# Half a gate set ahead of the first hybrid scores, a fused final norm, zero products in three pauses, and an earlier gating at the FFN ends

## The chip, the cores and the metric

The kernel is one program on one core of one Trainium2 chip. The metric is the device time of one execution in microseconds (us), of which three were taken. Its engines work side by side and each takes its instructions in the order in which they are written: TensorE (PE: matrix products and transposes, called turns here), VectorE (DVE), ScalarE (ACT), GpSimd (POOL) and SyncE (SP, which issues most transfers from memory). They wait for one another by semaphores.

## The reference, cut to what matters

256 tokens of width 1024, in float32, go through two blocks, each of them a first FFN, a mixing of tokens by two attentions, and a second FFN; then a final norm, one hybrid layer, and a mixture of 32 experts.

```python
for l in range(2):
    x = x + 0.5 * g1 * swiglu(modulate(x, sh1, sc1), ...)     # FFN of width 2816
    x = x + g2 * token_mix(modulate(x, sh2, sc2), ...)
    x = x + 0.5 * g3 * swiglu(modulate(x, sh3, sc3), ...)
x = rms_norm(x) * final_norm

h = modulate_2(x, norm1_w, shift1, scale1)                    # the hybrid layer
x_in, conv_b, conv_c, q, k, v, f_logit, gate_conv_l, gate_attn_l = split(h @ w_in)
p_a = (conv_b * causal_depthwise_conv(conv_c * x_in, conv_w)) @ w_out_conv
p_b = forgetting_attention(rmsnorm(q), rmsnorm(k), v, log_sigmoid(f_logit + b)) @ w_out_attn
x = x + gate1 * ((sigmoid(gate_conv_l) * p_a + sigmoid(gate_attn_l) * p_b) @ w_o)

h2 = modulate_2(x, norm2_w, shift2, scale2)                   # the router and the experts
group = argmax(h2 @ w_rg); the two best experts of that group, weighted by softmax
x = x + gate2 * sum over experts of weight * ((silu(h2 @ w_gate) * (h2 @ w_up)) @ w_down)
```

## The kernel before

Every weight matrix is streamed from memory through `raw`, three blocks of 2048 columns for 128 partitions. Each block is split in halves of 1024 columns into a rounded part `w_hi` (ACT, L518) and the remainder `w_lo` (DVE, L986). The activations are split likewise (`uT_hi`, `uT_lo`), and `mm3` (L1849 to L1851) makes one float32 product out of three: w_hi by the high part, w_lo by the high part, w_hi by the low part. Nearly all of PE's work is such triples of 128 by 512. The order of everything is written by hand, engine by engine; semaphores with running counts link the engines (`x_ready` counts finished halves of `x`, `xn_done` scaled halves, `split_done` converted halves of weights).

**Norms.** ACT squares each of the four 128 by 512 parts of `x` (L535, two token tiles t by two halves h) and sums them; DVE adds two sums (`rms_sum`, L999), ACT takes the root (L539), DVE inverts it (`rms_inverse`, L1004) and scales the tile (`rms_scale`, L1010, two halves). PE turns the scaled tile into `bank` (L1892, 16 turns of 128 by 128), ACT and DVE apply scale and shift and split it (L568, L571, L1053, L1058), and the column products begin. While a norm runs, PE has nothing to do; `norm` on PE begins with `keep_warm(16, ...)`, 16 bfloat16 products of zeros by zeros, 128 by 512, into a bank that is not in use (L1839).

**FFN ends.** Four times a DVE function `x_update_ffn` multiplies four accumulated banks by the gate (L1103, L1121), adds them to `x` (L1104, L1124), and starts the next norm. Just ahead of it stands `h_tile(1)` (L1085), the low part of the last hidden tile.

**Final norm.** After the second block `x` is scaled by its own norm into `xn` (L1010) and multiplied by the rows of `final_norm` (L1532, 128 by 1024 for each tile); then the hybrid layer's own norm follows on the result.

**Hybrid layer.** After four column units of 768 and the forget gates come four gate sets of 512 columns (set 1: `hyb_gates(1)`, 8 values of k by 2 token tiles by 3 products, 48 products), and four attention jobs. `sc_job(j)` makes the scores of job j on PE (L2072, L2073), DVE adds a mask (L1269), ACT takes exponentials (L642), later PE turns and multiplies by the values. The order on PE ahead of the first job is: turns of q, k, the conv inputs (L2125), a wait for `kh_ready` (ACT's evicted k) and `uc_ready` (DVE's copy L1610 of the turned conv input), scores of job 0, the whole of set 1, scores of job 1, half of set 2. ACT takes the sigmoid of set 1 (L795) after the exponentials of job 0; set 2 writes to one of set 1's banks and waits for that.

**Router.** PE turns the logits (L2415), DVE picks the groups (L1687 to L1699), PE counts (L2419 to L2422), DVE builds 0/1 matrices `picks` (L1712), and PE gathers the chosen tokens by products with them (L2431, 32 products). The results go through DVE (L1664, L1673) to the first expert products; DVE also splits expert weights in between (L1723).

Of the kernel before, what the change touches and what calls it, by code (L numbers as in the profile page):

```python
# [33 lines left out]
T = S // P  # L34
D = 1024
KD = D // P
DEPTH = 2
# [59 lines left out]
def program(nc, stream, experts, ada, c_rows, consts, vecs, layer_vecs, cmp_w1, fnorm, x_in, out):  # L97
    ctx = ExitStack()
    with ctx:
# [290 lines left out]
        def gate_column(n, k):  # L390
            return modf[:, 16 + 8 * (n % 2) + k:17 + 8 * (n % 2) + k]

# [118 lines left out]
        def _(act):  # L511
# [355 lines left out]
            def token_hi(t):  # L867
                act.wait_ge(xn_done, 4 * (q6 + 2) + 2 * t + 2)
                act.activation(xn_hi[:, t], xn[:, t], ACT.Copy).then_inc(xn_hi_done, 1)
# [101 lines left out]
        def _(dve):  # L971
# [116 lines left out]
            def last_unit(u, f):  # L1088
                split(u, (2,), LAST_UNIT)
                hidden(f, (0,))  # L1090
                h_tile(0, (hL_hi_done, f // FFN_UNITS + 1), hL_ready)
                hidden(f, (1,))
                h_tile(1, (hT_hi_done, f + 1), hT_ready)

            def x_half(n, t, h, done):
                if (t, h) == (0, 0):
                    dve.wait_ge(gate_ready, n * 2 + 2)
                if (t, h) == (1, 1):
                    dve.wait_ge(*done)
                else:  # L1100
                    dve.wait_ge(first_tile, 3 * n + 2 * t + h + 1)
                c = slice(h * 512, (h + 1) * 512)
                link(V.tensor_tensor(upd[:, t, h], ACC[2 * t + h][:, :], gate_bc[:, c], ALU.mult))  # L1103
                V.tensor_tensor(x[:, t, c], x[:, t, c], upd[:, t, h], ALU.add).then_inc(x_ready, 1)  # L1104

# [8 lines left out]
            def x_update_ffn(n, done):  # L1114

                for t, h in ((0, 0), (0, 1), (1, 0)):
                    x_half(n, t, h, done)
                rms_sum(n + 1, 0)
                dve.wait_ge(*done)
                links[0] += 1  # L1120
                V.tensor_tensor(upd[:, 1, 1], ACC[3][:, :], gate_bc[:, 512:1024], ALU.mult).then_inc(chain, 1)  # L1121
                rms_inverse(n + 1, 0)
                dve.wait_ge(chain, links[1] + links[0])
                V.tensor_tensor(x[:, 1, 512:1024], x[:, 1, 512:1024], upd[:, 1, 1], ALU.add).then_inc(x_ready, 1)  # L1124
                rms_scale(n + 1, 0)

            def ffn1(l, u0, f0, n):
# [44 lines left out]
                x_update_ffn(stage, (used[2], u0 + n + 1))  # L1172

            def ffn2(l, u0, f0, n):
# [46 lines left out]
                x_update_ffn(stage, (used[2], u0 + n + 1))  # L1221
# [304 lines left out]
            q6, n6 = 3 * DEPTH, 3 * DEPTH  # L1526
            dve.wait_ge(c_landed, DEPTH * 32 + 32)
            for t in range(T):
                if t > 0:
                    norm_tile(q6, t)  # L1530
                dve.wait_ge(xn_done, 4 * q6 + 2 * t + 2)
                V.tensor_tensor(x[:, t], xn[:, t], fn_bc, ALU.mult).then_inc(x_ready, 2)  # L1532
# [294 lines left out]
        def _(pe):  # L1827
# [55 lines left out]
            def norm(n, q):  # L1883
                keep_warm(16, GU[0][:, :])
                pe.wait_ge(x_ready, 4 * q + 4)
                for t in range(T):
                    for b in range(4):
                        if b % 2 == 0:
                            pe.wait_ge(xn_done, 4 * q + 2 * t + b // 2 + 1)
# [416 lines left out]
            norm(n6, n6 + 1)  # L2306
            for m in range(4):
# [65 lines left out]
            m.then_inc(b_psum, 1)  # L2373
            pe.wait_ge(kh_ready, 2)
            pe.wait_ge(uc_ready, 1)

            def first():
                pe.wait_ge(fcum_ready, 1)
                hyb_gates(1)
# [37 lines left out]

            pe.wait_ge(sel_ready, 1)
# [3 lines left out]
            pe.matmul(ACC[1][:, 0:4], ones, g_sel[:, 1], start=False, stop=True, skip_group_check=True).then_inc(count_psum, 1)  # L2422
            pe.wait_ge(gate_ready, 2 * n6 + 4)
# [271 lines left out]
```

## Time and profile before

| | |
|---|---|
| device time, median of 3 | 1802.78 us (1800.56 to 1805.46) |
| the profiled execution: its time | 1803.52 us |
| its span in the trace | 1801.7 us |
| mean granted TensorE clock over the span | 0.987 of full |
| PE busy | 1727.0 us, 96% |
| DVE, ACT busy | 1368.1 us (76%), 967.6 us (54%) |
| chain of work that ended last | PE 83%, DVE 9%, ACT 5% |

An engine is busy while an instruction of its own runs. A share near 100% on PE means that other engines' work hides behind it nearly everywhere; the chain's 9% of DVE and 5% of ACT are the places where it does not. The granted clock is the share of full speed at which TensorE was let run in a stretch; 0.50 and 1.00 are its two levels, 1.2 and 2.4 GHz.

### The profile page before, as it was taken

What the parts mean: (1) busy time and instruction counts of PE and PEld (TensorE: products, weight loads), DVE (VectorE), ACT (ScalarE), POOL (GpSimd) and SP (SyncE); (2) the same over time, 40 slices, a digit from 0 to 9 for tenths busy, and PEclk for the clock granted to TensorE, in tenths of its full rate; (3) what the DMA queues carried; (4) which work ended last, traced back from release to release, by engine and by line L of the source; (5) the groups of instructions that cost most, each with busy time, mean ns of one, the idle gap of its engine ahead of it and who ended that gap; (6) DMA issues with size and microseconds to landing.
All of it is one profiled execution on the core that took longest, in us unless ns stands there. A gap on an engine that the chain in (4) does not pass through costs nothing.

```text
span 1801.7 us, 24959 instructions
## 1 busy us (share of the span) xinstructions
PE 1727.0 (96%) x8653; PEld 1406.2 (78%) x8653; DVE 1368.1 (76%) x2069; ACT 967.6 (54%) x1471; POOL 47.0 (3%) x92
## 2 busy tenths in 40 slices
PE   5999999999999999999989999999899998999998
PEld 3788878787788878887878878888687876888886
DVE  6887777766876678777687578876767578999997
ACT  3444464664644454445546655444535547777775
POOL 0000000000000000000000000000000000000000
PEclk8999999999999999999999999999898999999999
DMA  8988754225577759886622348887373444999994
GB/s 362 355 329 307 297 198 147 71 95 209 208 282 249 266 193 340 301 310 231 234 82 106 112 169 306 343 306 276 143 296 114 187 164 147 382 353 354 369 353 164
DMA packets 61802, 437.43 MB, mean 243 GB/s; under 512 B 6816, under 2 KB 7328, under 8 KB 9504
## 3 DMA queue, kind: packets, MB, share of 16 engines
q1 hardware_dynamic: 47504, 339.27, 50.0%
q0 software_dynamic: 12672, 92.28, 13.7%
q10 hardware_dynamic: 1552, 4.89, 0.8%
q8 instruction: 47, 0.77, 0.2%
q14 instruction: 27, 0.22, 0.0%
HBM read 435.36 MB, written 1.05 MB: 242 GB/s over the span
## 4 chain that ended last, share of the span: by engine, by line
PE 83%; DVE 9%; ACT 5%; issue 1%; DMA 1%; ACTq 0%; SPq 0%; DVEq 0%
PE bank L1849 25%; PE bank L1850 24%; PE bank L1851 24%; DVE w_lo L986 2%; PE bank L2095 2%; ACT w_hi L518 1%; PE bank L2113 1%; DVE ada_w L1018 1%; PE bank L1939 1%; PE bank L2075 1%; DVE arena L1325 1%; PE bank L2073 1%; PE bank L2431 1%; ACT arena L535 1%; PE bank L2069 1%
## 5 line engine op out<-in xcount | busy, mean ns | idle before, releaser
L986 DVE TENSOR_TENSOR w_lo<-raw,w_hi 128x1024 fp32r<-128x1024 f32 x426 | 501.8, 1221 | 201.3 <-ACT w_hi L518 200.2
L518 ACT ACTIVATE w_hi<-raw 128x1024 fp32r<-128x1024 f32 x426 | 426.6, 1052 | 333.8 <-PE bank L1851 330.5
L1849 PE MATMUL bank<-w_hi,uT_hi 128*128 128x512 f32 (+2 forms) x1408 | 551.4, 392 | 22.4 <-DVE uT_lo L1342 13.4
L1850 PE MATMUL bank<-w_lo,uT_hi 128*128 128x512 f32 (+2 forms) x1408 | 539.2, 383 | 0.0
L1851 PE MATMUL bank<-w_hi,uT_lo 128*128 128x512 f32 (+2 forms) x1408 | 538.2, 382 | 0.0
L1849 PEld LDWEIGHTS bank<-w_hi,uT_hi 128*128 128x128 f32 x1408 | 266.9, 190 | 81.3 <-DVE uT_lo L1342 15.4
L1851 PEld LDWEIGHTS bank<-w_hi,uT_lo 128*128 128x128 f32 x1408 | 266.7, 189 | 52.1
L1850 PEld LDWEIGHTS bank<-w_lo,uT_hi 128*128 128x128 f32 x1408 | 267.3, 190 | 47.2
L1849 PE MATMUL bank<-w_hi,r_arena 128*128 128x512 f32 (+1 forms) x744 | 294.7, 396 | 5.0 <-DVE r_arena L1747 2.5
L1850 PE MATMUL bank<-w_lo,r_arena 128*128 128x512 f32 (+1 forms) x744 | 290.9, 391 | 0.0
L1851 PE MATMUL bank<-w_hi,r_arena 128*128 128x512 f32 (+1 forms) x744 | 289.8, 390 | 0.0
L1018 DVE CUSTOM_DVE_ANT_0 ada_w<-ada_w,cmpw 128x1024 f32<-128x1024 f32 x176 | 207.1, 1220 | 8.1 <-DMA ada_w<-ada_pairs 7.8
L1849 PEld LDWEIGHTS bank<-w_hi,r_arena 128*128 128x128 f32 x744 | 139.8, 188 | 37.4 <-DVE r_arena L1747 3.2
L1851 PEld LDWEIGHTS bank<-w_hi,r_arena 128*128 128x128 f32 x744 | 139.7, 188 | 29.6
L1850 PEld LDWEIGHTS bank<-w_lo,r_arena 128*128 128x128 f32 x744 | 140.0, 188 | 26.7
L993 DVE TENSOR_TENSOR w_lo<-raw,w_hi 128x1024 fp32r<-128x1024 f32 x94 | 110.9, 1222 | 9.0 <-ACT w_hi L526 7.1
L526 ACT ACTIVATE w_hi<-raw 128x1024 fp32r<-128x1024 f32 x94 | 94.1, 1052 | 14.3 <-PE bank L1851 14.3
L584 ACT ACTIVATE arena<-bank 128x256 f32<-128x256 f32 x88 | 33.8, 386 | 120.6 <-PE bank L1851 120.6
L488 POOL DMA_DIRECT2D ada_w<-ada_pairs x88 | 46.8, 532 | 1290.0 <-DVE mods_gate L1018 555.2
L993 DVE TENSOR_TENSOR w_lo<-ada_w,w_hi 128x1024 fp32r<-128x1024 f32 x60 | 70.6, 1222 | 4.8 <-ACT w_hi L526 3.9
L526 ACT ACTIVATE w_hi<-ada_w 128x1024 fp32r<-128x1024 f32 x64 | 64.1, 1053 | 7.6 <-PE bank L1851 7.6
L642 ACT ACTIVATE arena<-arena,stat 128x256 f32<-128x256 f32 (+1 forms) x112 | 49.4, 444 | 19.0 <-DVE stat L1274 18.9
(339 smaller groups left out, 1461.5 us busy)
## 6 DMA issues: line engine op xcount, KB each, us to landing
raw<-weight_stream SPq DMA_DIRECT2D x216, 1024.0 KB, 4.9
ada_w<-ada_pairs POOLq DMA_DIRECT2D x88, 1024.0 KB, 5.2
raw<-expert_blocks SPq DMA_DIRECT2D x48, 1024.0 KB, 4.8
ada_w<-expert_blocks SPq DMA_DIRECT2D x32, 1024.0 KB, 4.9
cmpw<-expert_blocks SPq DMA_DIRECT2D x16, 1024.0 KB, 5.0
arena<-ada_pairs SPq DMA_DIRECT2D x5, 1024.0 KB, 13.1
ada_w<-ada_pairs SPq DMA_DIRECT2D x3, 1024.0 KB, 13.4
cmpw<-compress_w ACTq DMA_DIRECT2D x2, 1024.0 KB, 7.9
```

The costliest lines, as they stand in the source:

```text
L488: pool.dma_start(ada_w[:, slot], ada[g]).then_inc(ada_landed[slot], 16)
L518: act.activation(w_hi[:, b], v, ACT.Copy).then_inc(hi_done, 1)
L526: act.activation(w_hi[:, b], v, ACT.Copy).then_inc(hi_done, 1)
L584: act.activation(act_g[:, t], GU[t][:, 0:F_UNIT], ACT.Silu).then_inc(silu_done, 1)
L642: e = act.activation(v, v, ACT.Exp, bias=nmax[j % 2][:, h:h + 1], accum_out=psum_row[j % 4][:, h:h + 1])
L986: V.tensor_tensor(w_lo[:, b], v, f32(w_hi[:, b]), ALU.subtract).then_inc(split_done, 1)
L993: V.tensor_tensor(w_lo[:, b], v, f32(w_hi[:, b]), ALU.subtract).then_inc(split_done, 1)
L1018: e = V.tensor_tensor_reduce(w[:, i], w[:, i], c, 1.0, 0.0, ALU.mult, ALU.add, dst[:, i:i + 1])
L1849: pe.matmul(dst, xh, w_hi[:, off:off + n], start=first, stop=False, skip_group_check=True)
L1850: pe.matmul(dst, xh, w_lo[:, off:off + n], start=False, stop=False, skip_group_check=True)
L1851: return pe.matmul(dst, xl, w_hi[:, off:off + n], start=False, stop=last, skip_group_check=True)
L2095: m = pe.matmul(HT[:, a * DH:(a + 1) * DH], pT[j % 2][:, kt, a], v, start=kt == 0, stop=kt == qt, skip_group_check=True)
```

## The change

It has five parts.

- Hybrid attention, PE: the first half of gate set 1 (k 0 to 3, 24 products) goes ahead of the waits for `kh_ready` and `uc_ready` and of job 0's scores; the second half stays behind those scores.
- Final norm, DVE: one instruction for each half, x times the inverse root times the row (`final_half`), takes the place of the scaling into `xn` and of the multiplication. The second tile's sum and inversion stand between these halves. The counts of `xn_done` drop by four from there on.
- The pause of that norm, PE: after the 16 zero products three times seven more, each seven released by `x_ready` (after the first, second and fourth half), and five more behind the turns.
- Router, PE: nine zero products ahead of the wait for the groups, eight ahead of the wait for the picks.
- FFN ends, DVE: the multiplication by the gate for the part (0, 0) goes ahead of `h_tile(1)`.

```diff
+        def scaled(q):
+            return 4 * (q - (q > 3 * DEPTH))
...
             def token_hi(t):
-                act.wait_ge(xn_done, 4 * (q6 + 2) + 2 * t + 2)
+                act.wait_ge(xn_done, scaled(q6 + 2) + 2 * t + 2)
...
-                h_tile(1, (hT_hi_done, f + 1), hT_ready)
-
-            def x_half(n, t, h, done):
+
+            def gated(n, t, h, done):
                 if (t, h) == (0, 0):
                     dve.wait_ge(gate_ready, n * 2 + 2)
                 if (t, h) == (1, 1):
                     dve.wait_ge(*done)
                 else:
                     dve.wait_ge(first_tile, 3 * n + 2 * t + h + 1)
+                links[0] += 1
+                V.tensor_tensor(upd[:, t, h], ACC[2 * t + h][:, :], gate_bc[:, h * 512:(h + 1) * 512], ALU.mult).then_inc(chain, 1)
+
+            def added(t, h):
+                dve.wait_ge(chain, links[1] + links[0])
                 c = slice(h * 512, (h + 1) * 512)
-                link(V.tensor_tensor(upd[:, t, h], ACC[2 * t + h][:, :], gate_bc[:, c], ALU.mult))
                 V.tensor_tensor(x[:, t, c], x[:, t, c], upd[:, t, h], ALU.add).then_inc(x_ready, 1)
+
+            def x_half(n, t, h, done):
+                gated(n, t, h, done)
+                added(t, h)
...
-            def x_update_ffn(n, done):
-
-                for t, h in ((0, 0), (0, 1), (1, 0)):
+            def x_update_ffn(n, f, done, last=False):
+
+                gated(n, 0, 0, done)
+                h_tile(1, (hT_hi_done, f + 1), hT_ready)
+                added(0, 0)
+                for t, h in ((0, 1), (1, 0)):
                     x_half(n, t, h, done)
                 rms_sum(n + 1, 0)
-                dve.wait_ge(*done)
-                links[0] += 1
-                V.tensor_tensor(upd[:, 1, 1], ACC[3][:, :], gate_bc[:, 512:1024], ALU.mult).then_inc(chain, 1)
+                gated(n, 1, 1, done)
                 rms_inverse(n + 1, 0)
-                dve.wait_ge(chain, links[1] + links[0])
-                V.tensor_tensor(x[:, 1, 512:1024], x[:, 1, 512:1024], upd[:, 1, 1], ALU.add).then_inc(x_ready, 1)
-                rms_scale(n + 1, 0)
+                added(1, 1)
+                if not last:
+                    rms_scale(n + 1, 0)
...
-                x_update_ffn(stage, (used[2], u0 + n + 1))
+                x_update_ffn(stage, f0 + n - 1, (used[2], u0 + n + 1), last=l == DEPTH - 1)
...
             q6, n6 = 3 * DEPTH, 3 * DEPTH
+            def final_half(t, h):
+                c = slice(h * 512, (h + 1) * 512)
+                V.scalar_tensor_tensor(x[:, t, c], x[:, t, c], rstd[:, t:t + 1], fn_bc[:, c], ALU.mult, ALU.mult).then_inc(x_ready, 1)
+
             dve.wait_ge(c_landed, DEPTH * 32 + 32)
-            for t in range(T):
-                if t > 0:
-                    norm_tile(q6, t)
-                dve.wait_ge(xn_done, 4 * q6 + 2 * t + 2)
-                V.tensor_tensor(x[:, t], xn[:, t], fn_bc, ALU.mult).then_inc(x_ready, 2)
+            dve.wait_ge(rstd_done, 2 * q6 + 1)
+            dve.wait_ge(x_ready, 4 * q6 + 2 + 2)
+            final_half(0, 0)
+            rms_sum(q6, 1)
+            final_half(0, 1)
+            rms_inverse(q6, 1)
+            dve.wait_ge(rstd_done, 2 * q6 + 2)
+            final_half(1, 0)
+            final_half(1, 1)
             dve.wait_ge(x_ready, 4 * (q6 + 2))
             norm(q6 + 1, n6, late=HYB_U0)
...
             def norm(n, q):
                 keep_warm(16, GU[0][:, :])
+                if q == 3 * DEPTH + 1:
+                    for h in (1, 2, 4):
+                        pe.wait_ge(x_ready, 4 * q + h)
+                        keep_warm(7, GU[0][:, :])
                 pe.wait_ge(x_ready, 4 * q + 4)
                 for t in range(T):
                     for b in range(4):
                         if b % 2 == 0:
-                            pe.wait_ge(xn_done, 4 * q + 2 * t + b // 2 + 1)
+                            pe.wait_ge(xn_done, scaled(q) + 2 * t + b // 2 + 1)
...
             norm(n6, n6 + 1)
+            keep_warm(5, GU[0][:, :])
...
             m.then_inc(b_psum, 1)
+            pe.wait_ge(fcum_ready, 1)
+            hyb_gates(1, range(4))
             pe.wait_ge(kh_ready, 2)
             pe.wait_ge(uc_ready, 1)
 
             def first():
-                pe.wait_ge(fcum_ready, 1)
-                hyb_gates(1)
+                hyb_gates(1, range(4, KD))
...
+            keep_warm(9, GU[0][:, :])
             pe.wait_ge(sel_ready, 1)
...
+            keep_warm(8, GU[0][:, :])
             pe.wait_ge(gate_ready, 2 * n6 + 4)
```

Line numbers differ between the two programs: L1849 to L1851 (`mm3`) are L1868 to L1870 after it, L2125 (a turn) is L2148, L2072 and L2073 (scores) are L2095 and L2096, L1839 (zeros) is L1858.

On PE, at the hybrid's first scores, the rows before were these: the last turns of the conv inputs, job 0's scores, and the first product of set 1.

```order
L2125 MATMUL bank<-cst,arena 128x128 x8
L2072 MATMUL bank<-r_arena 128x256
L2073 MATMUL bank<-cmpw 128x256
...
L1849 MATMUL bank<-w_hi,uT_hi 128x512
L1850 MATMUL bank<-w_lo,uT_hi 128x512
```

On PE, in the same place, they are now these; the three rows of a triple stand eight times ahead of the first scores.

```order
L2148 MATMUL bank<-cst,arena 128x128 x8
L1868 MATMUL bank<-w_hi,uT_hi 128x512
L1869 MATMUL bank<-w_lo,uT_hi 128x512
L1870 MATMUL bank<-w_hi,uT_lo 128x512
...
L2095 MATMUL bank<-r_arena 128x256
L2096 MATMUL bank<-cmpw 128x256
```

What moved is the eight rows of scores: behind 24 products.

On DVE, at the final norm, before: the last halves of `x`, the scaling into `arena` (which holds `xn`), the product with the row, and the second tile.

```order
L1124 TENSOR_TENSOR x<-x,arena 128x512
L1010 TENSOR_SCALAR arena<-x,stat 128x512 x2
L1522 MEMSET stat 128x1
L1532 TENSOR_TENSOR x<-arena 128x1024
L999 TENSOR_TENSOR stat<-stat 128x1
L1004 RECIPROCAL stat<-stat 128x1
L1010 TENSOR_SCALAR arena<-x,stat 128x512 x2
L1532 TENSOR_TENSOR x<-arena 128x1024
L999 TENSOR_TENSOR stat<-stat 128x1
```

On DVE, there now (L1110 adds, L1540 is `final_half`, L1002 and L1007 are the sum and the inversion):

```order
L1110 TENSOR_TENSOR x<-x,arena 128x512
L1533 MEMSET stat 128x1
L1540 SCALAR_TENSOR_TENSOR x<-x,stat,arena 128x512
L1002 TENSOR_TENSOR stat<-stat 128x1
L1540 SCALAR_TENSOR_TENSOR x<-x,stat,arena 128x512
L1007 RECIPROCAL stat<-stat 128x1
L1540 SCALAR_TENSOR_TENSOR x<-x,stat,arena 128x512 x2
L1002 TENSOR_TENSOR stat<-stat 128x1
```

Four products of 512 columns stand where four scalings and two products of 1024 columns stood.

## Rows read from the trace of the kernel before

**Rows 1.** The page: busy time per engine, and TensorE's granted clock in 40 slices.
```profile
PE 1727.0 (96%) x8653; PEld 1406.2 (78%) x8653; DVE 1368.1 (76%) x2069; ACT 967.6 (54%) x1471; POOL 47.0 (3%) x92
...
PEclk8999999999999999999999999999898999999999
```

**Rows 2.** Timeline of PE at the hybrid's start: start, duration, [idle before <-releaser].
```profile
1266.05 3.63 PE L1839 MATMUL bank<-zeros 128*128 128x512 bf16 x16
...
1275.32 3.65 PE L1892 MATMUL bank<-cst,arena 128*128 128x128 f32 x16 [5.65 <-DVE arena L1010]
...
1286.01 0.40 PE L1849 MATMUL bank<-w_hi,uT_hi 128*128 128x512 f32 x1
```

**Rows 3.** Windows: PE busy (count) first, granted clock third from last; hybrid's start, first FFN end.
```profile
1266.00:1269.70 3.70, 3.67 (x17) 1.47 (x16) 3.17 (x9) 2.86 (x9) 0.00 (x0) 1.00 0.40 142
...
1275.30:1279.00 3.70, 3.65 (x16) 3.15 (x16) 2.48 (x7) 1.37 (x5) 0.00 (x0) 0.50 0.00 0
...
235.60:238.60 3.00, 2.79 (x24) 2.35 (x22) 2.04 (x5) 1.37 (x3) 0.00 (x0) 1.00 0.00 0
```

**Rows 4.** Timeline of DVE at the final norm and the hybrid's first norm.
```profile
1268.27 0.67 DVE L1124 TENSOR_TENSOR x<-x,arena 128x512 f32<-128x512 f32 x1
...
1273.97 0.16 DVE L999 TENSOR_TENSOR stat<-stat 128x1 f32<-128x1 f32 x1
...
1276.44 0.88 DVE L1010 TENSOR_SCALAR arena<-x,stat 128x512 f32<-128x512 f32 x2
```

**Rows 5.** Groups by form: busy and mean ns of one multiply-and-multiply on 256 columns.
```profile
L1619 DVE SCALAR_TENSOR_TENSOR arena<-arena,vec 128x256 f32<-128x256 f32 x8 | 3.3, 480 | 0.1
```

**Rows 6.** Timeline of DVE, ACT and PE at the first FFN's end.
```profile
229.50 0.69 DVE L1104 TENSOR_TENSOR x<-x,arena 128x512 f32<-128x512 f32 x1
...
231.73 0.61 ACT L535 ACTIVATE arena<-x 128x512 f32<-128x512 f32 x1
...
236.14 0.88 DVE L1010 TENSOR_SCALAR arena<-x,stat 128x512 f32<-128x512 f32 x2
...
244.17 0.50 PE L1849 MATMUL bank<-w_hi,uT_hi 128*128 128x512 f32 x1
```

**Rows 7.** Timeline of PE around the first hybrid scores and gate set 1.
```profile
1371.85 0.35 PE L2072 MATMUL bank<-r_arena 128*128 128x256 f32 x1 [1.65 <-DVE arena L1610]
...
1378.26 0.79 PE L1849 MATMUL bank<-w_hi,uT_hi 128*128 128x512 f32 x1
...
1391.21 0.28 PE L2072 MATMUL bank<-r_arena 128*128 128x256 f32 x1
...
1394.86 0.50 PE L1849 MATMUL bank<-w_hi,uT_hi 128*128 128x512 f32 x1
```

**Rows 8.** Windows inside gate set 1, columns as in rows 3.
```profile
1378.20:1382.20 4.00, 4.00 (x10) 3.14 (x10) 4.00 (x7) 1.36 (x2) 0.00 (x0) 0.50 0.00 0
...
1382.20:1391.20 9.00, 9.00 (x40) 7.37 (x39) 6.45 (x11) 3.37 (x9) 0.00 (x0) 0.99 0.35 117
```

**Rows 9.** Timeline of DVE and ACT in the same stretch.
```profile
1381.20 1.65 DVE L1269 SCALAR_TENSOR_TENSOR arena<-bank,arena,cst 128x256 f32<-128x256 f32 x4
...
1386.24 1.28 ACT L795 ACT_TABLE_LOAD   x1
...
1391.41 1.09 ACT L795 ACTIVATE arena<-bank 128x512 f32<-128x512 f32 x2 [3.88 <-PE bank L1851]
```

**Rows 10.** Timeline of PE at the router and the gather.
```profile
1493.42 0.39 PE L2419 MATMUL bank<-arena,cst 128*128 128x8 f32 x2 [1.96 <-DVE arena L1697]
...
1496.41 0.76 PE L2431 MATMUL bank<-picks,xn_hi 128*128 128x512 f32 x1 [1.94 <-issue]
...
1508.13 0.47 PE L1849 MATMUL bank<-w_hi,r_arena 128*128 128x512 f32 x1 [1.60 <-DVE r_arena L1673]
```

**Rows 11.** Waits of DVE during the gather: us in total, times, longest.
```profile
DVE arena L1664 <- PE bank L2431: 2.2, 3, 1.0
```

**Rows 12.** Window of the gather's first products, columns as in rows 3.
```profile
1496.40:1501.60 5.20, 5.19 (x12) 4.11 (x13) 4.54 (x14) 1.72 (x4) 0.00 (x0) 0.50 0.01 3
```

More of the change, by code:

```diff
@@ L1171, in ffn1 @@
                 last_unit(u0 + n - 1, f0 + n - 1)
-                x_update_ffn(stage, (used[2], u0 + n + 1))
+                x_update_ffn(stage, f0 + n - 1, (used[2], u0 + n + 1))
             def ffn2(l, u0, f0, n):
@@ L1220, in ffn2 @@
                 last_unit(u0 + n - 1, f0 + n - 1)
-                x_update_ffn(stage, (used[2], u0 + n + 1))
+                x_update_ffn(stage, f0 + n - 1, (used[2], u0 + n + 1), last=l == DEPTH - 1)
             def merge(u0, m, stage, gates, following, between, more=True):
```

## The prediction

> **What bounds the kernel now.** I read the page first: PE is busy for 1727.0 of 1801.7 us and its granted clock is at its upper level in nearly all of the 40 slices; the reader is to see the three slices that stand at 8 [rows 1]. Outside them there is little to win that is not fewer products. Two of them, 1261 to 1306 and 1351 to 1396 us, lie past the second block; the first is the kernel's start, which the change leaves alone. So I read the timelines of PE and DVE there and at the router, where the change also works, for pauses of PE and the clock behind each.
>
> Three places answer. At the hybrid's start PE runs out of zero products at 1266.05 + 3.63 = 1269.68 and waits till 1275.32 for a scaled tile, 5.65 us [rows 2]; the turns behind the pause run at the lower level (0.50), while zero products just ahead of it ran at 1.00, and turns at the first FFN's end, without such a pause, ran at 1.00 too [rows 3]. In the attention PE waits 1.65 us, then runs job 0's scores and the first part of set 1 at the lower level. At the router two pauses of about 2 us stand ahead of a gather that begins at the lower level. In all three PE is what ends last afterwards.
>
> **The change part by part.** The sum is made against the profiled execution, 1803.52 us, with 1.8 us around its span; it is 0.74 above the median of 1802.78.
>
> *Final norm.* DVE adds the last part of x till 1268.27 + 0.67 = 1268.94, and reaches the first sum of the next norm at 1273.97, 5.03 us later [rows 4]. In between now stand four products by a scalar and a row, a sum, an inversion. The trace has no such product of 512 columns. One of 256 columns takes 0.48 us [rows 5], so twice that, 0.96, bounds it above; a plain 512-column addition takes 0.67 [rows 4], which bounds it below. I take 0.75, nearer to the addition, since a fixed part is counted twice in 0.96. Four of them are 3.0, and the sum between them about 0.16 as in [rows 4]: the next sum then starts at about 1272.1, 1.9 earlier (2.2 with 0.67, 1.0 with 0.96). The inversion waits for ACT's root, but behind the second product, by which time it is done. **−1.9.**
>
> *Zero products there.* Twenty-one more, at 3.63/16 = 0.227 us each [rows 2], are 4.8 us. The first seven start when the first product is out, near 1269.7, as the sixteen end; the next follow without a gap, and the last seven start behind the fourth half, at some 1272.7, and end near 1274.3. The first scaled half would be there near 1273.4, so its turns start late by up to 0.9; but the second tile comes at 1276.44 − 1.9 + 0.5 = 1275.0 at the earliest, and eight turns of the first fit ahead of it at full clock. I charge **+0.1**. What is bought is the clock: from the scaling of the second tile to the first product of k = 2 it was 1286.01 − 1276.44 = 9.57 us [rows 2, 4]; the same path, with the same shapes, at the first FFN's end was 244.17 − 236.14 = 8.03 [rows 6], at full clock. **−1.5.** The product of k = 2 waits for converted weights at either place, so no more than this is to be had. The five products behind the turns lie in the pause for ACT and DVE, at nothing; without that cover they would be 1.1.
>
> *Half a set ahead of the scores.* Before: scores of job 0 from 1371.85 to 1378.26, 6.41 us; set 1 till 1391.21; scores of job 1 till 1394.86, 3.65 us at full clock [rows 7]. Inside set 1 the first 4 us ran at 0.50, and then 40 products took 9.00, 0.225 each [rows 8]. Now the products can start where PE stopped, 1371.85 − 1.65 = 1370.2; their weights are converted, since no wait stood ahead of them at 1378.26. 24 products make 5.5 us (till 1375.7), the scores 3.65 (till 1379.4), the rest of the set 5.5 (till 1384.9), job 1's scores 3.65 (till 1388.6). The pause is filled, and nothing behind it is slow: PE reaches set 2 about 6.2 earlier. Who else must keep up: DVE's mask of job 0 starts at 1381.20 behind its own work, whether the scores are there at 1378.3 or 1379.4, and so ACT's exponentials and table load stay: the load ends at 1386.24 + 1.28 = 1387.5, and the sigmoids, which waited 3.88 us for PE, take 1.09, till 1388.6 [rows 9]. Set 2 needs their bank. Both chains meet at about 1388.75. **−6.1**; DVE and ACT have no slack left there, so what is lost in either counts from now on. Queued behind the moved products are the scores alone, and DVE would wait for those only if they came after 1381.2.
>
> *Router.* Nine zero products, 2.0 us, stand in a pause of 1.96, eight, 1.8, in one of 1.94 [rows 10]: up to 0.1 late in the first, nothing in the second. The gather's first 12 products then take 12 × 0.225 = 2.7 in place of 5.2 us [rows 8, 12], 2.5 earlier. DVE, which takes in the gather, waited for it 2.2 us in three pieces [rows 11]; when these are gone DVE is the chain, so 2.2 is the limit. First expert product at 1505.9 instead of 1508.13 [rows 10]. **−2.2.**
>
> *FFN ends.* The multiplication starts up to 0.7 earlier on DVE (the length of such an instruction, [rows 6]), but the next norm goes by ACT: at the first end the first half of x was ready at 229.50 + 0.69 = 230.19, and ACT, busy with a conversion and a table load, squared it from 231.73 [rows 6]. DVE would wait for it. **0**; if it paid in full, four times that, 2.8.
>
> *Sum.* −1.9 + 0.1 − 1.5 − 6.1 − 2.2 = −11.6, so 1803.52 − 11.6 = **1791.9 us**. The stages behind each place run on PE with hardly a pause, so the gains should carry to the end.
>
> A rule of the Trainium skill speaks against the second and third term. "TensorE: Matmul & The Clock Gate", Part 4, says that the full clock does not engage for transpose-mode work, which does not count as busy the same way. The trace agrees in one place, where 16 turns in 3.65 us did not lift the clock from 0.50, and not in the other, where 24 turns and products at 235.6 kept it at 1.00 [rows 3]. By that rule the turns ahead of set 1 would drop the clock, and the time would be that of the first rival.
>
> **The rivals.**
> 1. *The clock falls during the turns ahead of set 1 all the same.* The products moved up would then run at 0.50. If it recovers after 4 us, as inside set 1 [rows 8], 2 us of the 6.1 are lost: 1793.9. If it takes all of the 10.4 us from 1371.85 to 1382.2 that it took before [rows 7, 8], 5.2 are lost: 1797.1. For it: turns did not lift the clock [rows 3]. Against it: they kept it at 235.6, and now no pause follows them. 15%, near 1795.
> 2. *The zero products do not hold the clock.* They then take twice as long, 0.45 each, and PE is late itself: at the norm 21 of them are 9.5 us from 1269.7, so turns start at 1279.2 instead of 1275.32, though then without the saving of 1.9; at the router the 17 are 7.7 in 3.9 of pause. That is +3.9 + 3.8 − 6.1 = +1.6: 1805. Against it: at 1266 to 1269.7 they ran at 1.00 [rows 3]. 5%.
> 3. *The attention gives part back.* DVE or ACT, without slack at 1388.6, or weights not converted in time for set 2, keep 3 to 4 of the 6.1: about 1795. For it: both chains already end where PE's does; against it: ACT's sigmoids waited 3.88 us for PE alone [rows 9]. 12%.
> 4. *The other side: the clock stays down through all of set 1 and both jobs' scores.* At the lower level a product takes about 0.42 [rows 8] and a job's scores 6.41: 48 × 0.42 + 12.8 = 33.0 from 1370.2, so 1403.2 instead of 1394.86, +8.3; with −5.5 from the rest 1806.3, slower than before. It decides if the clock is low at 1370 and not lifted within about 28 us of such work; before, it was lifted after 10.4. 4%.
> 5. *The FFN ends pay in full:* 1789.1. 4%.
>
> **How the numbers follow.** My forecast has 60%, its own range 1789.5 to 1794 (the product's two bounds, 0.3 less or 0.9 more, a spread of the runs of about 2). A measurement of this kernel can tell about 0.3%, 5.4 us, from no change; faster thus means below 1797.4. The forecast, rivals 1, 3 and 5 lie there, 91%, less some 7% for their upper tails and a run that falls high: 0.84. Rivals 2 and 4 lie within 0.3% above, with those tails: 0.13; 0.03 for slower. The range 1788.5 to 1798 leaves out rivals 2 and 4 and small tails.
>
> **What would show it.** Right: granted clock 1.00 in the turns of the hybrid's start and in the first 12 gather products; the next norm's first sum 3.2 us behind the last addition; a first product of set 1 0.1 us behind the turns, at 0.225 a product, scores of job 0 in 3.65; set 2 some 18.5 us behind those turns; first expert product 9.5 us behind the start of the gather; FFN ends as long as before. Wrong: a pause of PE ahead of set 2 for ACT's sigmoid, products at 0.42 behind the turns, zero products that end after what they wait for, or a new wait for weights in set 2 or in the merge, which would give the 6.1 back.

## The result, and the profile after

The changed kernel takes 1794.44 us (median of 6, 1787.76 to 1798.63) against 1802.79 us (6, 1800.56 to 1805.46): ratio 0.9946, 95% interval 0.9933 to 0.9960, 0.54% faster. The forecast was 1791.9 us, range 1788.5 to 1798.0. The profiled execution took 1796.7 us, its span is 1795.0 us at a mean granted clock of 0.991.

The page of the changed kernel, busy time of the engines and the clock in 40 slices: the two later slices that stood at 8 [rows 1] stand at 9.

```profile
PE 1733.0 (97%) x8696; PEld 1407.6 (78%) x8696; DVE 1365.8 (76%) x2067; ACT 967.5 (54%) x1471; POOL 46.9 (3%) x92
...
PEclk8999999999999999999999999999999999999999
```

**Hybrid's start.** The timeline of PE:

```profile
1266.78 8.32 PE L1858 MATMUL bank<-zeros 128*128 128x512 bf16 x37
1274.93 1.91 PE L1915 MATMUL bank<-cst,arena 128*128 128x128 f32 x16
1276.68 1.24 PE L1858 MATMUL bank<-zeros 128*128 128x512 bf16 x5
1278.66 0.47 PE L1868 MATMUL bank<-w_hi,uT_hi 128*128 128x512 f32 x1 [0.74 <-DVE uT_lo L1061]
...
1283.24 0.50 PE L1868 MATMUL bank<-w_hi,uT_hi 128*128 128x512 f32 x1
```

and that of DVE (the last addition, the first fused half, the next norm's first sum, its second scaling):

```profile
1268.77 0.67 DVE L1110 TENSOR_TENSOR x<-x,arena 128x512 f32<-128x512 f32 x1
...
1269.58 0.75 DVE L1540 SCALAR_TENSOR_TENSOR x<-x,stat,arena 128x512 f32<-128x512 f32 x1
...
1272.62 0.16 DVE L1002 TENSOR_TENSOR stat<-stat 128x1 f32<-128x1 f32 x1
...
1275.09 0.88 DVE L1013 TENSOR_SCALAR arena<-x,stat 128x512 f32<-128x512 f32 x2
```

The pause of 5.65 us and the slow turns [rows 2] are gone: 37 zero products lead into 16 turns that take 1.91 us together. From the first zero product to the first product of k = 2 it is 16.46 us against 19.96 before [rows 2], 3.5 less.

**Attention.** The timeline of PE and ACT from the last turns of the conv inputs to the first product of set 2, which answers to [rows 7, 9]:

```profile
1366.41 1.10 PE L2148 MATMUL bank<-cst,arena 128*128 128x128 f32 x8 [0.34 <-ACT cmpw L837]
...
1367.26 0.48 PE L1868 MATMUL bank<-w_hi,uT_hi 128*128 128x512 f32 x1
...
1372.82 0.28 PE L2095 MATMUL bank<-r_arena 128*128 128x256 f32 x1
...
1382.09 0.28 PE L2095 MATMUL bank<-r_arena 128*128 128x256 f32 x1
...
1384.83 1.08 ACT L798 ACTIVATE arena<-bank 128x512 f32<-128x512 f32 x2
...
1386.02 0.57 PE L1868 MATMUL bank<-w_hi,uT_hi 128*128 128x512 f32 x1 [0.20 <-issue]
...
1426.62 0.48 PE L1868 MATMUL bank<-w_hi,r_arena 128*128 128x512 f32 x1
```

The last row is the first product of the merge, the stage behind the attention. In the trace of before, the start of the same turns and the merge's first product were these:

```profile
1369.10 1.10 PE L2125 MATMUL bank<-cst,arena 128*128 128x128 f32 x8 [0.34 <-ACT cmpw L834]
...
1430.88 0.48 PE L1849 MATMUL bank<-w_hi,r_arena 128*128 128x512 f32 x1
```

Set 2 starts 19.61 us behind the start of those turns; before it was 1394.86 − 1369.10 = 25.76 (the product is in [rows 7]). That is 6.15 less. ACT's sigmoid now ends at 1385.91, just ahead of set 2, and PE is idle for 0.20 there.

Then comes what the forecast did not have. Windows of the changed kernel; the columns are busy time and count of PE, PEld, DVE, ACT, POOL, then the granted clock, and DMA:

```profile
1274.90:1276.70 1.80, 1.80 (x18) 1.75 (x17) 1.43 (x4) 0.20 (x1) 0.00 (x0) 1.00 0.00 0
1367.30:1385.80 18.50, 18.50 (x74) 12.63 (x72) 17.87 (x33) 8.95 (x17) 0.00 (x0) 1.00 0.31 118
1386.00:1389.40 3.40, 3.38 (x9) 2.62 (x10) 3.37 (x6) 1.81 (x2) 0.00 (x0) 0.54 0.00 0
1393.20:1406.70 13.50, 13.50 (x78) 11.22 (x76) 6.22 (x12) 11.39 (x24) 0.00 (x0) 1.00 0.39 144
1406.80:1413.50 6.70, 6.70 (x17) 5.20 (x17) 5.43 (x9) 3.94 (x6) 0.00 (x0) 0.50 0.04 5
1492.10:1496.00 3.90, 3.87 (x17) 3.18 (x18) 3.69 (x13) 2.53 (x5) 0.00 (x0) 1.00 0.00 0
```

The clock is at its upper level in the turns, in half a set, the scores and the other half, and in the gather. But behind the scores of job 1 and the idle 0.20 us it falls for 3.4 us, and during the scores of job 3 for 6.7 us, there with PE busy without a break ahead of it (13.50 of 13.50 us). Such a stretch at the lower level is called a drop from here on. By the lengths and levels of these rows the two cost about 1.6 and 3.3 us (an estimate). From the turns' start to the merge's first product it is 60.21 us instead of 61.78: of 6.15 us gained at set 2, 1.57 are left.

**Router.** The timeline of PE, which answers to [rows 10], from the logits' turns on:

```profile
1486.87 0.31 PE L2440 MATMUL bank<-cst,arena 36*128 36x36 f32 x2
1487.11 2.12 PE L1858 MATMUL bank<-zeros 128*128 128x512 bf16 x9
...
1490.06 1.89 PE L1858 MATMUL bank<-zeros 128*128 128x512 bf16 x8
1492.13 0.47 PE L2458 MATMUL bank<-picks,xn_hi 128*128 128x512 f32 x1 [0.19 <-issue]
...
1501.41 0.47 PE L1868 MATMUL bank<-w_hi,r_arena 128*128 128x512 f32 x1 [1.59 <-DVE r_arena L1692]
```

From the gather's start to the first expert product it is 9.28 us instead of 11.72. From the logits' turns it is 14.54 instead of 16.98 (they start at 1491.15 in the trace of before), 2.4 less. DVE no longer waits for the gather.

**The books.** In the profiled pair the three places give 3.5 + 6.15 + 2.4 = 12.1 us. 4.6 go back behind set 2, and 0.7 before the hybrid layer, where this execution had clock drops near 383 and 937 us and that of before one near 72: 6.8, against a difference of the spans of 6.7. Span times (1 − clock) is 1801.7 × 0.013 = 23.4 us before and 1795.0 × 0.009 = 16.2 after, which comes near the difference of the spans. It does not show that the clock is all of it: the shorter final norm and the pause ahead of the scores (1.9 and 1.65 us) were idle time of PE, and kernel e1 below has a span 3.9 us shorter than before at the same clock, 0.987. Among executions of one kernel the two do go together: those of the changed kernel had spans from 1786.1 us at 0.996 to 1797.0 at 0.990.

### The profile page after: what moved, and what is told of

Read it like the earlier page. It is cut to its first block, busy times and chain, and to the rows that moved or that the text cites. A ratio compares the mean times of both kernels' runs of the same rounds, so it can differ in the third digit from the quotient of the medians.

```text
span 1795.0 us, 25042 instructions
## 1 busy us (share of the span) xinstructions
PE 1733.0 (97%) x8696; PEld 1407.6 (78%) x8696; DVE 1365.8 (76%) x2067; ACT 967.5 (54%) x1471; POOL 46.9 (3%) x92
## 4 chain that ended last, share of the span: by engine, by line
PE 84%; DVE 9%; ACT 5%; issue 1%; DMA 1%; ACTq 0%; SPq 0%; DVEq 0%
PE bank L1868 25%; PE bank L1869 24%; PE bank L1870 24%; DVE w_lo L989 2%; PE bank L2118 2%; ACT w_hi L521 1%; PE bank L2136 1%; PE bank L1858 1%; DVE ada_w L1021 1%; PE bank L1962 1%; PE bank L2098 1%; DVE arena L1336 1%; PE bank L2092 1%; PE bank L2096 0%; ACT arena L538 0%
## 5 line engine op out<-in xcount | busy, mean ns | idle before, releaser
L1868 PE MATMUL bank<-w_hi,uT_hi 128*128 128x512 f32 (+2 forms) x1408 | 552.4, 392 | 21.5 <-DVE uT_lo L1353 12.9
L1870 PE MATMUL bank<-w_hi,uT_lo 128*128 128x512 f32 (+2 forms) x1408 | 539.0, 383 | 0.0
L1868 PEld LDWEIGHTS bank<-w_hi,uT_hi 128*128 128x128 f32 x1408 | 267.5, 190 | 81.2 <-DVE uT_lo L1353 14.9
L1870 PEld LDWEIGHTS bank<-w_hi,uT_lo 128*128 128x128 f32 x1408 | 266.9, 190 | 52.3
L1868 PE MATMUL bank<-w_hi,r_arena 128*128 128x512 f32 (+1 forms) x744 | 294.6, 396 | 5.0 <-DVE r_arena L1766 2.5
L1870 PE MATMUL bank<-w_hi,r_arena 128*128 128x512 f32 (+1 forms) x744 | 289.9, 390 | 0.0
L1868 PEld LDWEIGHTS bank<-w_hi,r_arena 128*128 128x128 f32 x744 | 139.7, 188 | 37.4 <-DVE r_arena L1766 3.2
L1870 PEld LDWEIGHTS bank<-w_hi,r_arena 128*128 128x128 f32 x744 | 139.7, 188 | 29.5
L1858 PE MATMUL bank<-zeros 128*128 128x512 bf16 x239 | 56.7, 389 | 5.9 <-DMA cst<-shape_constants 5.9
## 6 DMA issues: line engine op xcount, KB each, us to landing
ada_w<-ada_pairs SPq DMA_DIRECT2D x3, 1024.0 KB, 13.5
```

The costliest lines, as they stand in the source:

```text
L1858: pe.matmul(dst, zeros[:, 0:P], zeros[:, 0:dst.shape[1]], start=True, stop=True, skip_group_check=True)
L1868: pe.matmul(dst, xh, w_hi[:, off:off + n], start=first, stop=False, skip_group_check=True)
L1870: return pe.matmul(dst, xl, w_hi[:, off:off + n], start=False, stop=last, skip_group_check=True)
```

## The experiments

Two theories stood after the result. **Theory 1:** the terms are right, and the drops behind set 2 are chance, as others are in other stages. **Theory 2:** the new order brings them, because PE now reaches stretches of scores, turns and value products at another moment. "Old order" is job 0's scores ahead of all of set 1, as before; "new order" is half of set 1 first. In the old order the clock is low from the pause ahead of the scores into set 1 [rows 8]; its return there is called the recovery. Each kernel below was run against before on its own chip; "turns to merge" is the time from the start of the last turns of the conv inputs to the merge's first product, in the trace of each.

**One part at a time.** Each has only its piece of the diff above; e12 is the change without the first of its five parts.

> Only the half gate set ahead of the first hybrid scores is made, all else as before. Theory 1 (the terms add up, and the 4.6 us given back later in the attention are chance drops of the clock): from the last turns of the conv inputs to the first product of set 2 the time falls from 25.8 to about 19.6 us, median 5 to 6 us below before, and drops of the clock behind set 2 are seen in some kernels and not in others. Theory 2 (the moved products themselves bring the drops at the scores of jobs 1 and 3): the same 6 us at set 2, but the granted clock falls to 0.50 behind the scores again, and the median is only 1 to 2 us below before.

> Only the fused final norm and its zero products are made. Theory 1: the last FFN product to the first product of k = 2 goes from 20.2 to about 16.7 us, granted clock 1.00 in the turns, median 3 to 4 us below before; the attention's pause and its slow scores stay as before. Theory 2 (drops come from the moved attention products): the same, and no drop in the later attention.

> Only the zero products in the router's two pauses are made. Both theories: the gather's first 12 products at full clock, logits' turns to first expert product 17.0 to 14.5 us, median about 2.4 us below before. A rival, that zero products do not hold the clock there, gives 17.0 to some 18.5 and a slower kernel.

> Only the earlier gating at the four FFN ends is made. Theory 1: ACT sets the next norm, so DVE waits longer for its squares (0.9 instead of 0.4 us) and the median stays within 1 us of before. Rival: it pays in full, 2 to 2.8 us below before.

> The whole change but the half gate set ahead of the first scores, which stays in the old order. Theory 2 (in the new order the later scores let the clock fall, in the old order they do not): no drop after the recovery inside set 1, as in the four traces of the old order so far; from the last turns of the conv inputs to the merge's first product 60 to 62 us; and the median only 1.5 to 4.6 us above the changed kernel's 1794.4 to 1794.9, so 1796 to 1799.5. Theory 1 (the drops are chance in either order): drops after set 1 in this trace too, or a median 6 us above, 1800 to 1801.

| kernel | median, us (n) | before there, us (n) | ratio, interval |
|---|---|---|---|
| e1, attention alone | 1799.68 (11) | 1803.75 (35) | 0.9980 (0.9967 to 0.9993) |
| e2, final norm and its zeros alone | 1801.75 (12) | 1803.75 (35) | 0.9990 (0.9975 to 1.0005) |
| e3, router alone | 1799.93 (12) | 1803.75 (35) | 0.9982 (0.9970 to 0.9995) |
| e4, FFN ends alone | 1805.92 (11) | 1803.75 (35) | 1.0009 (0.9994 to 1.0023) |
| e12, all but the attention | 1800.08 (12) | 1802.18 (17) | 0.9983 (0.9971 to 0.9995) |

The places do in each what they did together. e2: first zero product to k = 2, 16.69 us. e3: logits' turns to first expert product, 14.55. e1: set 2 after 21.02 us and not 19.6, as both theories had it, because of a drop already inside the second half of set 1 (from 1378.3 us); a second one follows from 1388.6 us, and turns to merge are 58.46 us, 3.3 less than before. The medians of e1 and e2 fell by 4.1 and 2.0 us, less than the changed kernel's gains in these places (6.15 up to set 2, 3.3 for the norm); for e2 the interval still holds the 3.3, for e1 it ends at 6.0 (1803.75 × 0.0033). e3's median fell by 3.8, more than the 2.4 of its place, which its interval holds.

e4's timeline of DVE, last FFN end:

```profile
1265.94 0.16 DVE L999 TENSOR_TENSOR stat<-stat 128x1 f32<-128x1 f32 x1 [0.87 <-ACT arena L535]
```

DVE waits 0.87 us for ACT's squares, as foreseen. From the first zero product to the first column product it is 7.63 us at the first end and 8.14 at the second, as before; at the last 14.09 against 14.32. The median's rise of 2.2 us is not told from none by its interval, and nothing in the trace speaks for it.

e12 tells on the order. Its window behind the recovery, columns as above:

```profile
1386.00:1430.00 44.00, 43.52 (x221) 34.99 (x220) 23.94 (x42) 25.67 (x48) 0.00 (x0) 1.00 0.36 139
```

No drop, as in the four other traces of the old order. Its median, though, is 5.2 to 5.6 above the changed kernel's two medians (1794.44, and 1794.87 in e6): above theory 2's 1796 to 1799.5, and at the lower end of theory 1's 1800 to 1801. The trace speaks for theory 2, the median for theory 1. So the size of what is given back is left open by the medians; the ratios put the worth of the moved half set in the full change at 5 to 7 us, in e1 at 4, with intervals of 2 to 3 us on each.

**Without the zero products** (the lines `keep_warm(7/5/9/8, ...)` taken out of the changed kernel):

```diff
-                if q == 3 * DEPTH + 1:
-                    for h in (1, 2, 4):
-                        pe.wait_ge(x_ready, 4 * q + h)
-                        keep_warm(7, GU[0][:, :])
...
-            keep_warm(5, GU[0][:, :])
...
-            keep_warm(9, GU[0][:, :])
...
-            keep_warm(8, GU[0][:, :])
```

> The whole change without its zero products (those of the final norm's pause, the five behind the turns, the seventeen of the router). Theory 1 (the zero products are what holds the clock): turns and first column products at the hybrid's start and the first 12 gather products at 0.50 again, 1.5 and 2.2 us lost, so a median 3 to 4 us above that of the changed kernel. Rival (the shorter norm and the moved products alone would have held it): clock 1.00 in both places, median within 1 us of the changed kernel.

1797.05 us (5), ratio 0.9964 (0.9951 to 0.9977). The timeline of PE at the hybrid's turns and the gather:

```profile
1270.67 3.65 PE L1911 MATMUL bank<-cst,arena 128*128 128x128 f32 x16 [3.57 <-DVE arena L1013]
...
1488.80 0.77 PE L2451 MATMUL bank<-picks,xn_hi 128*128 128x512 f32 x1 [1.94 <-issue]
```

and the windows of the two:

```profile
1270.70:1274.30 3.60, 3.60 (x16) 3.10 (x16) 2.43 (x7) 1.27 (x5) 0.00 (x0) 0.50 0.00 0
1488.80:1493.60 4.80, 4.80 (x11) 3.79 (x12) 4.13 (x14) 1.71 (x4) 0.00 (x0) 0.50 0.01 3
```

The fused norm cuts the pause to 3.57 us, and the clock falls all the same; the turns take 3.65 us again and the gather starts slow. So the zero products hold the clock, and all traces agree: at the hybrid's start the clock is low in all five without them (before, e1, e3, e4, e5) and in none of the nine with them, and at the gather in all five without them (before, e1, e2, e4, e5) and in none of the nine with them. Without them the median is 2.2 to 2.6 us higher, less than the 3 to 4 expected, with intervals that overlap. Why it is less is not shown; e5's trace has no drops in the mixing stages, where the changed kernel's first trace has three, but its second (e6, below) has none either.

**The changed kernel once more.**

> The changed kernel once more, unaltered, for a second trace. Theory 1 (chance drops): other places than 380, 935, 1386 and 1407 us show drops in part, the span less the clock's deficit is again near 1778 us, and single executions lie between 1787 and 1799. Theory 2 (the moved products bring the drops): a drop behind the scores of job 1 or job 3 again.

1794.87 us (6), ratio 0.9956 (0.9942 to 0.9970). Near 383, 937 and 1003 us there is no drop this time, and one near 72; behind set 2 there is one again, at 1404 us, in the scores of job 3, and none behind those of job 1. The first part is theory 1's, the second theory 2's: that a drop comes in the new order repeats, and behind which scores does not.

**Scores among gate products.** In the hybrid layer, the scores of a job and the gate products beside them are interleaved:

```diff
+                        if amid:
+                            amid[2 * p + i]()
...
-                        sc_job(j0, jobs, j + 1)
-                        beside(j)
+                        sc_job(j0, jobs, j + 1, amid(j) if amid else ())
+                        if not (amid and j):
+                            beside(j)
...
-                hyb_gates(1, range(4, KD))
+                hyb_gates(1, (4, 5))
...
+                if j == 0:
+                    return [lambda: hyb_gates(1, (6,)), lambda: None, lambda: hyb_gates(1, (7,)), lambda: None]
...
+                return [lambda i=i: chunk(i) for i in range(4)]
```

`amid` is called behind each fourth of a job's scores; `chunk(i)` makes the products of one k of set 2 or 3.

> The changed kernel with the scores of hybrid jobs 1, 2 and 3 spread among the gate products beside them (a fourth of a job's scores, then one k, and so on), the same instructions in number. Theory 2 (runs of scores without dense products between them let the clock fall now that PE reaches them at another moment): no drops between 1376 and 1425 us, deficit 2 to 4 us smaller, median 2 to 4 us below the changed kernel. Theory 1: drops as often as before, there or elsewhere, median within 1 us.

1795.26 us (6), ratio 0.9961 (0.9948 to 0.9974): no gain, where theory 2 expected 2 to 4 us, and turns to merge 61.09 us. There is no drop from 1376 to 1414 us, as theory 2 had it, but the waits of PE from 1350 to 1440 us show why it does not pay (us in total, times, longest):

```profile
PE bank L2121 <- DVE arena L1302: 2.3, 1, 2.3
PE bank L2095 <- DVE arena L1280: 0.7, 1, 0.7
```

Job 3's scores end so late that the last value products wait 2.3 us for DVE, and right behind that wait the clock falls once. The next kernel spreads less: job 1 half its scores, k 7, the other half; job 2 as here; job 3 half, one k, half, three k.

> The changed kernel with scores spread among gate products so that no value product waits: job 1's first half, one k, second half; job 2's fourths with a k behind each; job 3's first half, one k, second half, three k. The 3 us of new waits seen where all three jobs were spread should be gone (PE's wait of 2.3 us for DVE ahead of the last value products, 0.7 ahead of job 1's scores). Theory 2 (scores without dense products between them let the clock fall): from the last turns of the conv inputs to the merge's first product 55 to 57 us against 57.1 to 60.2, median 2 to 3 us below the changed kernel. Theory 1 (chance): 57 to 60 as before, median within 1 us.

1792.28 us (6), ratio 0.9941 (0.9926 to 0.9956). The windows of this kernel that answer to the second to fifth of the changed kernel's:

```profile
1367.30:1385.80 18.50, 18.50 (x75) 12.63 (x73) 17.80 (x33) 8.94 (x17) 0.00 (x0) 1.00 0.31 118
1386.00:1422.00 36.00, 35.41 (x191) 29.35 (x192) 21.11 (x38) 23.74 (x47) 0.00 (x0) 1.00 0.42 160
```

The clock stays up through all of it, and turns to merge take 55.63 us: with the same products, 6.15 less than before, so that here the whole gain at set 2 reaches the merge. The median is 2.2 to 2.6 below the changed kernel's, at the foot of theory 2's 2 to 3; the intervals overlap, the traces do not. The table goes up to the merge; drops are counted behind the recovery in the old order, behind the start of set 1 in the new.

| order in the attention | kernels | drops | turns to merge, us |
|---|---|---|---|
| old | before, e2, e3, e4, e12 | none in 5 | 60.27 to 61.81 |
| new | changed, e1, e5, e6, e8, e10 | in all 6 | 56.92 to 60.21 |
| new, scores of jobs 1 to 3 spread evenly | e7 | one, behind the wait of 2.3 us | 61.09 |
| new, scores spread as in e9 | e9, e11 | none in 2 | 55.63, 55.68 |

The idle 0.20 us ahead of set 2 is a rival for the changed kernel's first drop: there PE waits for ACT's sigmoid. e10, described below, speaks against it. Its windows from behind the start of the turns up to a drop in job 1's scores, and behind it:

```profile
1363.50:1381.70 18.20, 18.20 (x75) 12.67 (x72) 17.54 (x33) 8.63 (x17) 0.00 (x0) 1.00 0.32 121
1381.80:1385.10 3.30, 3.27 (x9) 2.32 (x8) 3.22 (x8) 2.24 (x3) 0.00 (x0) 0.50 0.00 0
```

The clock fell while the scores ran, with PE busy in all of the 18.20 us ahead; and e9 has an idle 0.18 us ahead of set 2 and no drop.

**The mixing stages' pauses.** The same two means, products moved into a pause and zero products, where drops were seen in some traces, near 318, 385, 937 and 1003 us:

```diff
+                        if j == 9:
+                            keep_warm(6, SPARE[:, :])
                         pe.wait_ge(w_evac_a, l * 9 + 5 + j // 3)
-                    for i, k in GATE_CHUNKS[j]:
+                    for i, k in GATE_CHUNKS[j][(1 if j == 0 else 0):]:
...
+                def ahead():
+                    pe.wait_ge(km_ready, l * 4 + 4)
+                    gate_chunk(*GATE_CHUNKS[0][0])
+
-                jobs_run(l * NJ, l * 6, JOBS, beside, ending=lambda: turn_o((0, 1)))
+                jobs_run(l * NJ, l * 6, JOBS, beside, first=ahead, ending=lambda: turn_o((0, 1)))
```

> The changed kernel with the two mixing stages treated alike: the first gate chunk of six products goes ahead of the scores of job 1 (a pause of 1.7 us there), six zero products ahead of the wait for ACT's sigmoid at job 9 (a pause of 1.6 us). If the drops near 318, 385, 935 and 1000 us come from these pauses: none there any more, and with 1.3 us of pause filled by real work in each of two layers a median 4 to 6 us below the changed kernel. If they do not come from the pauses: 2 to 3 us below at most.

1788.66 us (5), ratio 0.9918 (0.9906 to 0.9931), 6.2 below the changed kernel on the same chip, and the intervals do not meet; expected were 4 to 6 if the pauses bring the drops. The timeline of PE in the first layer, scores of job 0, the moved chunk, scores of job 1:

```profile
317.99 1.14 PE L2098 MATMUL bank<-arena 64*128 64x256 f32 x8
319.49 0.50 PE L1868 MATMUL bank<-w_hi,uT_hi 128*128 128x512 f32 x1 [0.36 <-DVE cmpw L1498]
...
321.10 1.14 PE L2098 MATMUL bank<-arena 64*128 64x256 f32 x8
```

Of the pause of 1.7 us 0.36 is left, and no drop is in either mixing stage of this trace, nor of those of e10 and e11, which have the same edit. Of the eleven traces without it seven have one to three there and four (e1, e5, e6, e7) none, so the median says more here than one trace.

**And the first FFN's pause**, eleven zero products ahead of the loop of the first FFN:

```diff
                 down(u0, f0)
+                if nn == 0:
+                    keep_warm(11, SPARE[:, :])
```

> The kernel of the mixing pauses with eleven zero products more, ahead of the loop of the very first FFN, where PE waits 2.6 to 3.2 us for DVE and the clock then fell near 72 us in seven of nine traces. If that pause is the cause: no drop there, 1 to 1.7 us below the kernel of the mixing pauses. If the zeros end late or the drop comes from the stretch before: the same or 0.5 us slower.

1789.65 us (5), ratio 0.9925 (0.9911 to 0.9939). The window just behind that pause, first in e8, then here:

```profile
70.00:75.00 5.00, 4.72 (x16) 4.01 (x17) 5.00 (x8) 0.60 (x1) 0.53 (x1) 0.66 0.81 269
```

```profile
70.00:75.00 5.00, 4.65 (x23) 3.92 (x24) 5.00 (x8) 0.60 (x1) 0.53 (x1) 1.00 0.81 288
```

The drop is gone in the trace, as in that of e11; of the twelve traces without this edit nine have it. The median does not show a gain (0.99 above e8, intervals overlapping).

**All of it.**

> All of it: the changed kernel, the mixing pauses, the first FFN's pause and the spread scores. By theory 2 the gains add: 4 to 5 us (mixing) + 1 to 1.7 + 2 to 3 below the changed kernel, near 1785 to 1787. By theory 1 the spread scores add nothing: 1787 to 1789.

1786.02 us (5, 1785.34 to 1788.53), ratio 0.9909 (0.9895 to 0.9922): faster than before and than the changed kernel (0.9946, 0.9933 to 0.9960). From e10 it differs by the spread scores alone: on the same chip the median is 3.63 us lower, and four of its five executions lie below all five of e10's, though the intervals of the ratios still overlap. By its expectation this is theory 2's time (1785 to 1787) and not theory 1's (1787 to 1789). The window over all but the start and the end:

```profile
45.00:1780.00 1735.00, 1703.37 (x8604) 1388.19 (x8622) 1336.76 (x2009) 950.57 (x1442) 45.58 (x87) 1.00 0.65 242
```

The clock is at 1.00 throughout, and the five executions lie within 3.2 us, where those of the changed kernel lie within 10.9.

## Why the prediction was right, and where it was not

Time, sign and range held; the likeliest value was 2.5 us too low. The median also lies 0.4 us above the range that the forecast gave to its own case (1789.5 to 1794), next to the "about 1795" of rival 3. The range was wide enough for a loss that the prediction did not name, but single executions, from 1787.76 to 1798.63, reach beyond both of its ends, so that chance had a part in it. Step by step:

- *Final norm, −1.9.* The new instruction takes 0.75 us, the value chosen between 0.67 and 0.96. Last addition's end to the next sum: 3.18 us instead of 5.03. Right.
- *Zero products there, +0.1 and −1.5.* From the second scaling to k = 2 it is 8.15 us, against 8.03 expected and 9.57 before: −1.42 together. e5 shows that they, and not the shorter pause, hold the clock. Right.
- *Attention, −6.1.* At set 2: −6.15, with ACT's sigmoid just ahead of it, as worked out. The step that failed is the sentence that "the gains should carry to the end": between the first scores and the merge the new order has clock drops in six of six traces, and the old one none in five. Of the 6.1 there were left 1.6 (changed kernel) to 4.9 us (e10) at the merge, and all of it in e9, without drops. "Nothing behind it is slow" held for the changed kernel up to set 2; in e1 and e5 a drop came right behind job 0's scores, and the gain at set 2 was 4.7 to 4.9. Rival 3 had the outcome (part given back) and the wrong cause: it named DVE, ACT and weights. That runs of scores without dense products between them have a part in the drops is shown by e9 and e11, where spreading them took the drops away with no product less. They are not enough by themselves: the old order has the same run of job 1's scores, 3.65 us, and no drop behind it in five traces. Why is not settled, and the medians leave open how much the drops cost in the mean.
- *Router, −2.2.* −2.44, 0.2 more than DVE's waits, which the prediction took as the limit; these waits are gone, as was said. Right.
- *FFN ends, 0.* At the first three nothing; at the last 0.23. Right.
- *Rival 1* did not happen: the turns ahead of set 1 kept 1.00 in every trace of the new order, so the rule of the Trainium skill weighed there ("TensorE: Matmul & The Clock Gate", Part 4), by which they would have cost 2 to 5 us, is not borne out in this place. *Rival 2:* the zeros held the clock everywhere. *Rival 4:* no. *Rival 5:* no, by e4.

The prediction also read from the page that there was little to win outside the slices that stand at 8. e8 won 6.2 us in slices that stand at 9: a drop of 3.4 us inside a slice of 45 us leaves it at 9. And the forecast took the profiled execution as typical for what it does not touch. Executions differ by whole drops, each some 1.7 us (an estimate: 3.4 us at half the clock), near 72, 318, 385, 937 and 1003 us; that made the medians of single parts (e1, e2, e4) poor measures, where the traces' distances were good ones.

## What to carry to other kernels

Where PE is the bound, a change's gain is held only as long as the clock is: look with windows at every stretch behind the edit in which PE is busy with small products, scores or transposes, and not at its pauses alone. Real work moved into a pause fills it and took the drops away here, zero products only hold the clock, and both pay if they fit; spreading small products among dense ones costs nothing as long as the small ones' consumers still get them in time (e7 against e9). Compare such kernels by distances within traces and by the granted clock, since single executions differ by more than a part is worth.

## What the runs showed of the hardware

The granted clock fell to 0.50 with PE busy without a break ahead: in e10 from 1381.7 us, behind 18.2 us of unbroken work, the last 3.4 of it scores, and in the changed kernel from 1406.7 us, behind 13.5 us of turns, value products, scores and gate products. "Busy" in the profile is therefore no sign that the clock is safe. The Trainium skill ("TensorE: Matmul & The Clock Gate", the section "HAM oscillation — how this bites in real kernels") names idle gaps of PE as what lets the clock fall; here it fell without one. In e5 the gather started at 0.50 behind a pause of 1.94 us, with another of 1.96 shortly ahead of it and little work of PE between the two. Pauses of 1.6 to 1.7 us in the mixing stages had a drop behind them in one execution of the changed kernel and not in the other (e6).
